# Three weight passes for the feed-forward, one per token chunk, with the samples' steps moved behind the join

## What is computed

```python
h = rmsnorm(x, P['g_norm1'][l]) * (1.0 + sc1) + sh1
mix, states = token_mix(h, st_hg[l], st_ssm[l], st_conv[l], st_wkv[l], st_shift[l], lb_all[l], l, P)
x = x + (g1 * mix).astype(x.dtype)
h = rmsnorm(x, P['g_norm2'][l]) * (1.0 + sc2) + sh2
ff = (jax.nn.silu(h @ P['w_gate'][l]) * (h @ P['w_up'][l])) @ P['w_down'][l]
x = x + (g2 * ff).astype(x.dtype)
y = rmsnorm(x, P['g_final']).astype(x.dtype)
```

## Time and profile before

| | us |
|---|---|
| median of 3 runs | 1986.81 |
| lowest and highest | 1985.63 and 1986.86 |
| the profiled execution | 1994.82 |
| its span, first to last instruction | 1993.1 |
| PE busy in it | 1673.1 (84%) |
| VectorE busy | 978.0 (49%) |
| ScalarE busy | 589.7 (30%) |

### The profile page before, as it was taken

One profiled execution on the slowest core, in us unless ns is written; L12 is line 12 of the kernel. 1 busy time (PEld: TensorE's weight loads), 2 busy tenths in 40 slices (PEclk: granted clock), 3 DMA queues, 4 the chain that ended last, 5 costly groups with the idle time before them and its releaser, 6 DMA issues.

```text
span 1993.1 us, 32180 instructions
## 1 busy us (share of the span) xinstructions
PE 1673.1 (84%) x13599; PEld 1519.4 (76%) x13599; DVE 978.0 (49%) x2112; ACT 589.7 (30%) x1055; POOL 254.5 (13%) x333
## 2 busy tenths in 40 slices
PE   4898888887988627587788877999979999999995
PEld 2898777876877513256677777988869999999995
DVE  5405436665543346766666734555553333433334
ACT  2214223312422233123433434433342212222222
POOL 3500001110100032012233331000000000000000
PEclk9899889888987758568888999999989999999998
DMA  8110001010100055242221233433312131222311
GB/s 298 37 53 22 22 16 39 29 40 26 58 30 29 8 170 162 75 146 73 61 62 54 69 118 88 121 101 107 118 56 82 56 96 56 76 84 61 92 47 54
DMA packets 199302, 149.23 MB, mean 75 GB/s; under 512 B 6479, under 2 KB 187200, under 8 KB 198136
## 3 DMA queue, kind: packets, MB, share of 16 engines
q1 hardware_dynamic: 188482, 120.67, 20.1%
q0 software_dynamic: 7728, 23.27, 3.4%
q10 hardware_dynamic: 2950, 3.24, 0.5%
HBM read 134.03 MB, written 13.18 MB: 74 GB/s over the span
## 4 chain that ended last, share of the span: by engine, by line
PE 69%; DVE 19%; ACT 6%; issue 3%; DMA 2%; POOL 0%; SPq 0%; POOLq 0%; DVEq 0%; ACTq 0%
PE bank L1241 17%; PE bank L1242 17%; PE bank L1243 17%; PE bank L1180 2%; PE bank L1593 1%; PE bank L1592 1%; PE bank L1428 1%; ACT WHI L1765 1%; PE bank L1429 1%; PE bank L1377 1%; PE bank L1384 1%; PE bank L1439 1%; PE bank L1386 1%; PE bank L1524 1%; ACT PS L1993 1%
## 5 line engine op out<-in xcount | busy, mean ns | idle before, releaser
L1241 PE MATMUL bank<-HBH,WHI 128*128 128x328 f32 (+1 forms) x832 | 262.8, 316 | 14.8 <-DVE HBL L2321 10.1
L2204 DVE TENSOR_TENSOR WLO<-RAW,WHI 128x1024 fp32r<-128x1024 f32 (+4 forms) x149 | 152.1, 1023 | 238.4 <-ACT WHI L1765 237.9
L1765 ACT CAST WHI<-RAW 128x1024 fp32r<-128x1024 f32 (+4 forms) x210 | 188.0, 898 | 254.3 <-PE bank L1243 243.9
L1242 PE MATMUL bank<-HBL,WHI 128*128 128x328 f32 (+1 forms) x832 | 261.1, 314 | 0.0
L1243 PE MATMUL bank<-HBH,WLO 128*128 128x328 f32 (+1 forms) x832 | 260.1, 313 | 0.0
L1241 PE MATMUL bank<-HHI,WHI 128*128 128x344 f32 x624 | 215.6, 345 | 11.8 <-DVE HLO L2417 6.5
L1242 PE MATMUL bank<-HLO,WHI 128*128 128x344 f32 x624 | 207.3, 332 | 0.0
L1243 PE MATMUL bank<-HHI,WLO 128*128 128x344 f32 x624 | 206.6, 331 | 0.0
L1002 POOL TENSOR_TENSOR WLO<-RAW,WHI 128x1024 fp32r<-128x1024 f32 (+1 forms) x61 | 131.1, 2152 | 506.3 <-ACT WHI L1765 506.2
L1241 PEld LDWEIGHTS bank<-HBH,WHI 128*128 128x128 f32 x832 | 158.6, 191 | 16.5 <-issue 16.3
L1243 PEld LDWEIGHTS bank<-HBH,WLO 128*128 128x128 f32 x832 | 158.7, 191 | 0.0
(11 more groups left out here) (554 smaller groups left out, 3157.5 us busy)
## 6 DMA issues: line engine op xcount, KB each, us to landing
RAW<-in_w_gate SPq DMA_DIRECT2D x44, 512.0 KB, 3.9
RAW<-in_w_up SPq DMA_DIRECT2D x44, 512.0 KB, 3.9
RAW<-in_w_ada SPq DMA_DIRECT2D x32, 512.0 KB, 4.2
RAW<-in_w_in SPq DMA_DIRECT2D x26, 512.0 KB, 3.8
ADAW<-in_w_ada SPq DMA_DIRECT2D x8, 1024.0 KB, 19.9
RAW<-in_w_out SPq DMA_DIRECT2D x16, 512.0 KB, 4.3
RAW<-in_w_down SPq DMA_DIRECT2D x32, 256.0 KB, 2.7
RAW<-in_w_down SPq DMA_DIRECT2D x16, 384.0 KB, 3.5
```

Source lines behind the costliest of these rows:

```text
L1241: mm(bank[:, 0:w], whi[:, k, :], hi_k, start=(k == 0), stop=False)
L1242: mm(bank[:, 0:w], whi[:, k, :], lo_k, start=False, stop=False)
L1765: a.copy(w_split(i)[0][:, 0:nk, :], RAW[u % NRAW][:, 0:nk, :]).then_inc(w_hi, 1)
L2204: v.tensor_tensor(wlo[:, 0:nk, :], RAW[u % NRAW][:, 0:nk, :], whi[:, 0:nk, :].bitcast(F32), ALU.subtract).then_inc(w_lo, 1)
```

## The change

Each chunk gets a pass of its own over the feed-forward weights, so three passes. The units of a pass are laid out one after another in `dense_plan`: chunk 1's eight `out` units are dealt out in pairs over chunk 0's groups 2 to 5, ahead of the `down` units of each; chunk 2's stand ahead of the last `down` group of chunk 1. Chunks 1 and 2 have groups of 7, 7 and 8, and one more `gate` and `up` pair stands ahead of each group's `down` units. The items of a norm stand between two `down` or `gate` units of another chunk (`BEHIND2`, `EARLY`), in the order 3, 4, 6, 5, 7, 8. `PLAN3` is gone. The mixer blocks hold no sample steps; each step stands between two units behind the join. A split is emitted right ahead of the unit before its own (`emit`), with two units' distance behind the join, and there are three slots. The states of the samples are loaded behind the join, into two buffers that are used twice. All sample rows of TensorE move from bank 2 to bank 6. Chunk 0's second buffers (`HAH`, `HAL`) serve chunk 2 too, and `MIXR` holds the hidden tiles of every chunk.

```diff
-GROUPS = [[4, 4, 4, 4, 3, 3], [6, 6, 5, 5]]
+GROUPS = [[4, 4, 4, 4, 3, 3], [7, 7, 8], [7, 7, 8]]
+AFTER = 2
-NORMS = [3, 6, 4, 5, 7, 8]
+NORMS = [3, 4, 6, 5, 7, 8]
...
+    units += out[0]
+    f = 0
+    for g, n in enumerate(GROUPS[0]):
+        units += pairs(0, f, f + n)
+        f += n
+        if g >= AFTER:
+            units += out[1][2 * (g - AFTER):2 * (g - AFTER) + 2]
+        units += downs(0, g)
+    for c in (1, 2):
+        begun = end = 0
+        for g, n in enumerate(GROUPS[c]):
+            end += n
+            ahead = min(end + 1, FF // P)
+            units += pairs(c, begun, ahead)
+            begun = ahead
+            if c == 1 and g == len(GROUPS[c]) - 1:
+                units += out[2]
+            units += downs(c, g)
...
-    NRAW, NSPL1, NSPL3 = 3, 2, 4
+    NRAW, NSPL1, NSPL3 = 3, 2, 3
...
+        BEHIND2 = {('out', (1, KT - 1)): [('sum', 4), ('scaled', 4), ('rest', 4)],
+                   ('out', (2, KT - 1)): [('sum', 5), ('scaled', 5), ('rest', 5)]}
+        EARLY = {('down', (0, len(GROUPS[0]) - 1, KT - 1)): [('sum', 6), ('normed', 6)] + [
+                     ('ya', (i, h)) for i in range(3) for h in range(2)],
+                 ('down', (1, len(GROUPS[1]) - 1, KT - 1)): [('sum', 7), ('normed', 7)] + [
+                     ('ya', (i, h)) for i in range(3, 5) for h in range(2)]}
...
+        def emit(item, ahead=1):
+
+            if item[0] == 'half' and item[1][1] != 1:
+                while NEXT[0] <= min(SIDX[UNITS_OF(item[1][0])] + ahead, len(SPLIT) - 1):
+                    PLAN2.append(('split', NEXT[0]))
+                    NEXT[0] += 1
+            PLAN2.append(item)
...
-                if samples and item[0] != 'mb_out':
-                    PLAN2.append((samples.pop(0), 0))
...
-        PLAN2 += [('join', 0), ('mixsplit', 1), ('mixsplit', 2)]
-        fill(len(ffn), True)
+        PLAN2.append(('join', 0))
+        joined_at = len(PLAN2)
+        while ffn:
+            item = ffn.pop(0)
+            if item[0] in ('pause', 'stop'):
+                continue
+            emit(item, 2)
+            if item[0] == 'half' and item[1][1] != 0 and samples:
+                PLAN2.append((samples.pop(0), 0))
...
-                    if arg == 5:
+                    if arg in (4, 5, 6, 7):
                         tables(SILU_SET)
```

More of the change, by code:

```diff
@@ L132, in dense_plan, with pairs, downs @@
     n1 = len(units)
-    ends = []
-    for part, groups in enumerate(GROUPS):
-        units += [('out', t) for t in range(8)]
-        f = 0
-        for g, n in enumerate(groups):
-            for i in range(n):
-                units += [('gate', f), ('up', f)]
-                f += 1
-            units += [('down', (part, g, d)) for d in range(KT)]
-        ends.append(len(units))
-    return units, n1, ends[0]
+    out = [[('out', (c, t)) for t in range(KT)] for c in range(NCH)]
+    def pairs(c, f0, f1):
+        return [(kind, (c, f)) for f in range(f0, f1) for kind in ('gate', 'up')]
+    def downs(c, g):
+        return [('down', (c, g, d)) for d in range(KT)]
+    units += out[0]
[16 more added lines that the diff above has]
+            units += downs(c, g)
+    return units, n1
 def kernel_program(nc, ins, outs):
@@ L799, in kernel_program @@
         late = list(range(QP1, QP2))
-        ffn = [('mixsplit', 0), ('split', n1s), ('pause', 0)]
-        up_ends = [u for u in range(N1, N2 - 1) if UNITS[u][0] == 'up' and UNITS[u + 1][0] == 'down']
-        for q in range(QP2, QP2A):
-            ffn += [('split', i) for i in splits_at.get(q, [])]
-            if unit_k(UNITS_OF(q)) == KT:
+        ffn = [('mixsplit', 0), ('pause', 0)]
+        queued, later = [], []
+        AT = {('gate', (0, sum(GROUPS[0][:AFTER]))): [('stop', 0)],
+              ('out', (1, 0)): [('stop', 0), ('mixsplit', 1)], ('gate', (1, GROUPS[1][0] + 1)): [('mixsplit', 2)]}
+        NOW = {('out', (0, KT - 1)): [('sum', 3), ('pause', 0), ('scaled', 3), ('pause', 0), ('rest', 3), ('pause', 0)]}
+        for g in range(AFTER):
+            NOW[('up', (0, FIRST_F[0][g + 1] - 1))] = [('pause', 0)]
+        BEHIND2 = {('out', (1, KT - 1)): [('sum', 4), ('scaled', 4), ('rest', 4)],
[4 more added lines that the diff above has]
+                     ('ya', (i, h)) for i in range(3, 5) for h in range(2)]}
+        for q in range(QP2, len(QUANTA)):
+            unit = UNITS[UNITS_OF(q)]
+            ffn += AT.get(unit, [])
+            if unit_k(UNITS_OF(q)) == KT and q < QJ:
                 ffn += [('half', (q, 0)), ('half', (q, 1))]
@@ L851, in kernel_program @@
                         PLAN2.append(('adt', 2))
-        assert not late and not samples
+        assert not late
         PLAN2.append(('mix_final', 0))
```

303 lines of the change are left out of this document (145 added, 158 removed).

## The result

The changed kernel takes 2003.43 us (median of 5 executions, 1995.76 to 2009.5), against 1986.86 (1985.63 to 1988.86): ratio 1.0076, interval 1.0046 to 1.0106. In a second set the same two kernels gave 2004.48 and 1988.52: 1.0075 (1.0053 to 1.0097). I had forecast 1958.3. So the change is slower by 15 us where it should have been faster by 28.5; the median misses the forecast by 45 us. Three executions on record lie far above the others of their kernel (2442.3 us of the kernel before, 2072.81 of `e2_lodve`, 3130.14 of `e11_nosamp_splits`), and every ratio and its interval leave them out.

What follows compares the result with a forecast made beforehand. TensorE was taken as the bound behind the join and VectorE in block 1. Terms −40 + 4 + 9.5 + 5 + 3 − 10 = −28.5 us gave a median of 1958.3, range 1938 to 1982.

Steps and rivals of the forecast that it cites:

- What bounds the kernel: Behind the join TensorE is the bound; block 1, with the large sample steps, is bound by VectorE.
- a. Steps leave the blocks: Mixer blocks 0 to 2: without sample steps −40 us, of which 28.7 in block 1; bounds −20 to −46.
- the small steps: Blocks 0 to 2: some ten in each, 0.4 us apiece, 3.8 us for a block, 11.3 in all.
- c and d. What the steps cost behind the join: TensorE waits 11.8 us at `sh6`, 4.4 at `sm4` and `sm5`, 1 at `sm8`; the 32 steps' own work adds 5.
- b. The splits: Before the join, blocks 3 to 7: splits emitted one mixer stage later cost +4 us; bounds −5 to +12.
- One of my signs of being wrong: The prediction is wrong if blocks 3 to 7 are longer by more than 12 us in all.
- c. The norms: Behind the join: TensorE waits 10.5 us at norm 4, 9.1 at norm 5, 6.5 at norms 6 and 7.
- f. The tail: After the last products only chunk 2's norm and 15 matmuls are left: 23.9 us instead of 33.7, −10.
- Transfers: Chunks 1 and 2 load weights twice, 152 more units' loads from 1400 to 1960 us; costed at nothing.
- the slower one that I had: Long passes: `RAW` loads land late under twice the traffic; landing in 9 us costs +50: 2008 us; chance 0.06.
- blocks keep their time: Blocks 0 to 2 lose only 20 us, or steps cost TensorE 1.5 us each behind the join: 1978; chance 0.18.

Runs made afterwards that it cites:

- e2_lodve: The changed kernel with every `WLO` before the join computed by VectorE instead of GpSimd, place of the splits unchanged: 1994.27 us, ratio 1.0033 to the kernel before.
- e11_nosamp_splits: The changed kernel without the samples' steps and with the splits of blocks 3 to 7 where they stood before: 1948.28 us, ratio 0.9819 to the kernel before.
- e7_before_nosamp: The kernel before without the samples' 32 steps: 1962.87 us, ratio 0.9857 to the kernel before.
- e8_apart: The changed kernel with TensorE's product with `SO` three dense units behind VectorE's instructions of step `sh6`: 2005.13 us, ratio 1.008 to the kernel before.
- e1_splits: The changed kernel with splits in mixer blocks 3 to 7 back at the end of the stage ahead: 1989.6 us, ratio 0.9994 to the kernel before.

## Why the prediction was wrong

The main step that failed is the price of the samples' steps behind the join, and next to it the place of the splits. By my own steps, with the measured sizes (differences by the ratios, each known to some 6 to 11 us; stretches by the table above):

- **What bounds the kernel** was right: block 1 was bound by VectorE, it is as long as its neighbours now, and the long passes run at full pace with VectorE at 0.52, as worked out.
- **a. Steps leave the blocks**: −40 forecast, −31 in the trace of the changed kernel and −37 in the second one, −28 by `e7_before_nosamp`. The 28.7 us for block 1 are there. What was too large is the 11.3 us for the small steps, an estimate that took every matmul, transposition and short vector operation as in somebody's way: the traces leave 2 to 9 us for them.
- **c and d. What the steps cost behind the join**: 11.8 + 4.4 + 1 + 5 = 22.2 us forecast, 28 in the trace behind the join, 2.6 more in the tail, and 36 by the ratios. The wait for `SO` was 13.8 us against 11.8, and those for the splits at `sm4` and `sm5` are 2.2 + 1.4 against 4.4, so the queue was reckoned well. But I priced waits at single places, where VectorE is behind over the whole stretch: `e8_apart` takes the wait for `SO` away and gains nothing. On top of it the granted clock is 0.79 in this stretch, where it is 1.00 without steps. I had costed no loss of clock anywhere. With a, this turns a gain of 18 us into a loss of 8: 26 us of the miss.
- **b. The splits**: +4 forecast with an upper bound of 12, and 16 measured by `e1_splits`. This is the step whose mechanism I had named and mis-sized. I took half a cast for each split, but the split stands in the rows of ScalarE and GpSimd behind a mixer stage, and that stage waits for another engine (4.03 us at 884), so a whole link of the mixer's chain comes in front of the cast, plus 2.4 us for GpSimd's `WLO`, which I had priced as VectorE's 1.22. Here too the clock adds its part, 0.87 against 0.92. 12 us of the miss. One of my signs of being wrong was blocks 3 to 7 longer by more than 12 us in all; it came, with 19.3 up to the 960th matmul.
- **c. The norms**: norm 4's wait is 10.0 + 1.2 us (10.5 forecast), norm 5's 9.0 at 1713 us and 0.8 (9.1 forecast): right, in mechanism and size. Around each come 2 to 3 us more, with the lower clock. Norms 6 and 7 with the transposes had 9.5 us; the waits alone are 4.8 + 4.0 + 2.8, and the stretches from 1446 to 1515 and from 1733 to 1798 take 20 us longer than their 386 and 383 dense matmuls at a pace of 147 and 150 ns. A wait of 4.0 us for `MIXR` at 1953, ahead of chunk 2's last `down` units, I did not have at all.
- **f. The tail**: 21.7 us forecast behind the last matmul, 24.3 measured. The table load is there with 1.28. GpSimd's last drain, 3.00 us instead of 0.79, makes 2.2 of the other 2.6; without the steps the tail is 21.7, as forecast.
- The three passes, the norms and the tail together are worth −8 by `e11_nosamp_splits` against `e7_before_nosamp`, where my terms gave −14.7: 7 us of the miss by the ratios, 9 by the traces. 26 + 12 + 7 is the 45. That it comes out so closely is luck, given how well each part is known.
- **Transfers**: chunks 1 and 2 load 152 units in all, where the two-chunk pass had 84; so 68 loads are more, and not 152. Nothing in the sum hangs on it.
- **The rivals**: the slower one that I had (loads that land late) did not happen; 3.9 us stayed 3.9. The "blocks keep their time" rival was wrong for the blocks, where 31 us or more came off and not 20. The 1.5 us for each sample step that it had as a mere figure lies above the 0.9 to 1.1 us that 28 to 36 us make for each of 32, and it was not a wait at each step. The range ended at 1982, since I let the terms vary one at a time around a sum of gains. The small steps, the splits and the steps behind the join all erred to the same side. For the last two the rows show why: each was a cover that I took from a stretch's free time and not from who stands in front in the queue.
